# Convolution LayerNorm and swish moved ahead of the output projection, the conv half first, and the first convolution tile as VectorE multiply-adds, in a two-layer hybrid diffusion backbone

## The chip, the cores and the metric

The kernel runs on one core of one Trainium2 chip. The metric is the device time of one execution in microseconds (us); lower is better. Of the kernel before, three runs gave a median of 1693.96 us (1691.78 to 1694.18), and one more execution was profiled.

## The reference

Two layers, each with an attention group and a convolution group side by side, then one output projection and a feed-forward part (SwiGLU). There are 512 latent tokens and 256 context tokens; the second layer updates the latent tokens alone. Cut to what matters here:

```python
h = modulate(rmsnorm(x, g_mix[l]), sh1, sc1)
q, k, v, u = split_in(h @ w_in[l])                    # 512 | 128 | 128 | 1024 columns
q, k = rope_2d(q, ...), rope_2d(k, ...)
a_out = latent_attention(q, k, v, k_c, v_c, sink[l])  # 8 heads, 2 KV heads, window of 128
cv_out = conv_module(u, w_dw[l], b_dw[l], ln_g[l], ln_b[l])
x = x + gt1 * (concat([rmsnorm(a_out, g_a), rmsnorm(cv_out, g_c)]) @ w_o)
h2 = modulate(rmsnorm(x, g_ffn[l]), sh2, sc2)
x = x + gt2 * swiglu(h2, w_gate_up[l], w_down[l])

def conv_module(u, w_dw, b_dw, ln_g, ln_b):           # 512 channels, 31 taps per channel
    z = u[..., :512] * sigmoid(u[..., 512:])
    z = depthwise_conv(z, w_dw) + b_dw
    return silu(layernorm(z, ln_g, ln_b))
```

## The kernel before, in words

Features lie on the 128 partitions and tokens along the free dimension, so a width of 1024 is 8 tiles and the convolution group is 4 tiles (CT). A tile is 768 columns wide in layer 0 (latent and context) and 512 in layer 1. Every float32 product is made of three fp32r matmuls: high weights by high activations, high by low, low by high. ScalarE makes the high part of the weights (`split_high`, L643) and VectorE the low part (`split_low`, L902), both in two buffers; the next block of TensorE needs both. SyncE's queue brings the weights, 512 KB a block.

The order is written out by hand for each engine. Per layer, TensorE (L395) runs these phases:
- **u** (8 blocks), the convolution group's input. VectorE's `u_pair` (L1101) makes the gated z. GpSimd's `shift_z` (L1291) issues 16 DMAs for each tile that lay out shifted copies of z. `conv_tile` (L461) then does the depthwise convolution of a tile as matmuls over those copies. `CONV_AFTER` (L329) puts the four tiles behind u blocks 5, 6 and 7 and qkv block 0. ScalarE copies the sums out with the bias (`conv_copy`, L694).
- **qkv** (6 blocks): keys, four tiles of queries, values. For each, VectorE scales, splits weights and turns (`rope`, L1056), ScalarE copies the high part of the queries (L787, L788), and VectorE subtracts the low part (L1129, L1131).
- **attention** (L518, L700, L996): 48 units (a head by a block of 128 queries) in layer 0 and 32 in layer 1. TensorE computes scores, turns the probabilities and multiplies by the values, ScalarE does the exponential and the copy of the turned probabilities, and VectorE the row maximum and the division.
- **oa** (`out_phase`, L503): 8 tiles of the output projection over the attention half, 4 k-tiles each. The statistics of the convolution's LayerNorm and of both group norms are issued between its tiles (STAT_AFTER, L331). The sums over features are VectorE's (`add_square`, L908), the sums over partitions and the broadcasts are TensorE's (`stat_tokens`, L415, `stat_broadcast`, L423), the root is ScalarE's (L664), the reciprocals on a diagonal are VectorE's (`diagonal`, L922).
- **ob**: the 8 tiles over the convolution half. For oa as for ob, VectorE scales each product by the gate and the group's inverse root (`gate_out`, L985) and GpSimd adds it to x (L1331).
- **gu0, dn0, gu1, dn1, gu2, dn2**: the feed-forward part. The first gu0 block starts on the tiles of x as they become ready and carries the statistics of the norm before it (n2).

`Chain.link` (L119) makes an engine wait for its own last instruction before the next one, which is how dependent VectorE instructions are ordered.

## Time and profile before

| | us |
|---|---|
| median of 3 runs | 1693.96 (1691.78 to 1694.18) |
| profiled execution | 1693.07, of which the traced span is 1691.3 |
| TensorE matmul busy | 1594.6 |
| VectorE, ScalarE, GpSimd busy | 797.1, 571.7, 129.9 |

The mean granted TensorE clock is 0.977 of full speed. In the trace, layer 0 runs u from 52 to about 170 us, qkv to 231, attention to 325.6, oa and ob to 436.9, the feed-forward part to 1031. Layer 1 follows: u to 1099, qkv to 1148, attention to 1224.7, oa and ob to 1300.5, the feed-forward part to the end. PE is the matmul, PEld the weight load, DVE VectorE, ACT ScalarE, POOL GpSimd. In the clock column 1.00 is 2.4 GHz and 0.50 is 1.2 GHz.

### The profile page before, as it was taken

The numbers are of one execution on the slowest core, as the hardware profiler recorded it, in microseconds if no ns is written. First come the engines' busy times: TensorE is split into PE (matmuls) and PEld (weight loads), VectorE is DVE, ScalarE is ACT, GpSimd is POOL, SyncE is SP. The second block draws the span as 40 slices with busy tenths as digits, with TensorE's granted clock in tenths as the row PEclk, the third lists the DMA queues.
The fourth block names the chain that finished last, engine by engine and source line by source line (L and its number), as shares of the span: only waits on it lengthen the run. The fifth ranks groups of instructions, "written<-read, shape, count | busy, mean of one in ns | idle before, by whom it ended". The sixth has DMA issues, their size and how long they took to land.

```text
span 1691.3 us, 25398 instructions
## 1 busy us (share of the span) xinstructions
PE 1594.6 (94%) x9996; PEld 1288.5 (76%) x9996; DVE 797.1 (47%) x1468; ACT 571.7 (34%) x890; POOL 129.9 (8%) x182
## 2 busy tenths in 40 slices
PE   4899989888999999999999999997988999999997
PEld 1666665576788878888788878685566998998995
DVE  1521578786534323343233455267786443443445
ACT  2411257743343211222112233126754541222222
POOL 0133000033100000000000002410032000000000
PEclk9999999998899999999999999998999999999998
DMA  7574420011122432223421354520012323233322
GB/s 317 201 216 128 162 100 2 1 38 38 51 62 62 137 137 100 62 62 134 140 96 63 102 173 150 139 77 29 1 38 63 100 87 99 88 97 90 91 83 87
DMA packets 41180, 165.02 MB, mean 98 GB/s; under 512 B 6160, under 2 KB 6544, under 8 KB 34960
## 3 DMA queue, kind: packets, MB, share of 16 engines
q1 hardware_dynamic: 35856, 148.69, 26.6%
q0 software_dynamic: 5248, 15.27, 3.3%
q8 instruction: 53, 0.87, 0.2%
q14 instruction: 23, 0.19, 0.0%
HBM read 150.77 MB, written 2.10 MB: 90 GB/s over the span
## 4 chain that ended last, share of the span: by engine, by line
PE 82%; DVE 5%; issue 5%; ACT 3%; POOL 3%; DMA 1%; SPq 1%; DVEq 0%; ACTq 0%; POOLq 0%
PE banks L446 66%; PE banks L474 4%; PE banks L546 3%; PE banks L558 2%; PE banks L571 2%; POOL x L1331 2%; PE banks L404 2%; DMA x<-in_xT 1%; DVE ssum L913 1%; PE banks L420 1%; PE banks L433 1%; ACT w_high L650 1%; DVE w_low L906 1%; ACT prob L712 0%; POOL z_shifted L1305 0%
## 5 line engine op out<-in xcount | busy, mean ns | idle before, releaser
L446 PE MATMUL banks<-h_high,w_high 128*128 128x258 f32 (+2 forms) x2048 | 499.9, 323 | 29.4 <-DVE h_low L935 17.6
L446 PE MATMUL banks<-h_low,w_high 128*128 128x258 f32 (+2 forms) x2048 | 491.2, 319 | 0.0
L446 PE MATMUL banks<-h_high,w_low 128*128 128x258 f32 (+2 forms) x2048 | 490.5, 318 | 0.0
L650 ACT ACTIVATE w_high<-raw 128x1024 fp32r<-128x1024 f32 (+1 forms) x178 | 185.1, 1040 | 668.3 <-PE banks L446 660.1
L446 PEld LDWEIGHTS banks<-h_high,w_high 128*128 128x128 f32 x2048 | 323.0, 192 | 79.6 <-issue 41.9
L446 PEld LDWEIGHTS banks<-h_low,w_high 128*128 128x128 f32 x2048 | 322.8, 191 | 28.1 <-issue 0.7
L446 PEld LDWEIGHTS banks<-h_high,w_low 128*128 128x128 f32 x2048 | 322.0, 191 | 27.6
L906 DVE TENSOR_TENSOR w_low<-raw,w_high 128x1024 fp32r<-128x1024 f32 (+1 forms) x178 | 218.2, 1226 | 247.0 <-ACT w_high L650 243.0
L949 DVE COPY shift_product<-banks 128x2 f32<-128x2 f32 x116 | 18.5, 159 | 431.7 <-PE banks L446 407.3
L446 PE MATMUL banks<-ff_high,w_high 128*128 128x512 f32 (+1 forms) x528 | 162.5, 362 | 0.5 <-DVE ff_low L1235 0.5
L446 PE MATMUL banks<-ff_low,w_high 128*128 128x512 f32 (+1 forms) x528 | 160.4, 358 | 0.0
L446 PE MATMUL banks<-ff_high,w_low 128*128 128x512 f32 (+1 forms) x528 | 160.3, 358 | 0.0
L446 PEld LDWEIGHTS banks<-ff_high,w_high 128*128 128x128 f32 x528 | 86.9, 188 | 33.4 <-issue 17.6
L446 PEld LDWEIGHTS banks<-ff_high,w_low 128*128 128x128 f32 x528 | 87.1, 188 | 16.0
L446 PEld LDWEIGHTS banks<-ff_low,w_high 128*128 128x128 f32 x528 | 87.1, 188 | 15.9
L950 DVE TENSOR_TENSOR tmp<-banks,inv_root 128x768 f32<-128x768 f32 (+1 forms) x116 | 95.1, 820 | 0.1
L1331 POOL TENSOR_TENSOR x<-x,tmp 128x768 f32<-128x768 f32 (+1 forms) x32 | 61.2, 1923 | 401.9 <-DVE tmp L992 401.9
L546 PE MATMUL banks<-k_stacked,q_stacked 128*128 128x384 f32 (+2 forms) x224 | 61.9, 383 | 11.9 <-DVE tmp L950 5.7
L1305 POOL DMA_DIRECT2D z_shifted<-z_padded x128 | 62.8, 499 | 130.4 <-issue 54.4
L474 PE MATMUL banks<-z_shifted,w_conv 128*32 128x512 f32 (+1 forms) x768 | 70.4, 521 | 0.8 <-DMA w_conv<-in_w_conv 0.8
L1005 DVE TENSOR_REDUCE row_max<-banks 128x1 f32<-128x512 f32 (+2 forms) x80 | 55.3, 691 | 29.2 <-PE banks L546 28.7
L858 ACT ACTIVATE ff_high<-tmp 128x768 f32 (+3 forms) x44 | 32.5, 740 | 97.9 <-DVE tmp L1231 97.9
(129 smaller groups left out, 1234.5 us busy)
## 6 DMA issues: line engine op xcount, KB each, us to landing
raw<-in_w_gu SPq DMA_DIRECT2D x88, 512.0 KB, 3.6
ada_raw<-in_w_ada SPq DMA_DIRECT2D x21, 1024.0 KB, 5.2
raw<-in_w_dn SPq DMA_DIRECT2D x32, 512.0 KB, 3.6
raw<-in_w_mix SPq DMA_DIRECT2D x28, 512.0 KB, 5.8
ada_in_ff<-in_w_ada SPq DMA_DIRECT2D x12, 1024.0 KB, 5.0
raw<-in_w_out SPq DMA_DIRECT2D x16, 512.0 KB, 3.6
ada_first<-in_w_ada SPq DMA_DIRECT2D x7, 1024.0 KB, 12.9
z_shifted<-z_padded POOLq DMA_DIRECT2D x64, 101.4 KB, 2.7
```

The costliest lines, as they stand in the source:

```text
L404: last = mm(bank[32 * q:32 * q + 32, ADA, :], cond[:, k, :], tile[:, 512 * q:512 * q + 512], start=(k == 0), stop=(k == DT - 1), tile_posi ...
L446: last = mm(bank[:, 2 * slot + bk, 0:b - a], weights[w][:, k0_w + k, :], rhs[:, k0_rhs + k, a:b], start=(k == 0 and n == 0), stop=(k == kt ...
L474: last = mm(bank[QC * q:QC * q + QC, BC + bk, 0:b - a], wD[:, j, g, QC * q:QC * q + QC], zr[j][:, q, SH * g + a:SH * g + b], start=(g == 0 ...
L546: last = mm(wide[:, at:at + w], lhs, rhs, start=in_bank[m] not in in_bank[:m], stop=in_bank[m] not in in_bank[m + 1:], skip_group_check=True)
L558: last = nc.tensor.transpose(wide[:, 512 * PTB + P * m:512 * PTB + P * m + P], probs[u % 4][:, P * m:P * m + P], ident[:])
L571: last = mm(bank[HD * odd:HD * odd + HD, BC + n % 2, 0:2 * P], V[:, keys[m], HD * g:HD * g + HD], PT[:, n % 2, m, 2 * odd:2 * odd + 2, :]. ...
L650: f(wH[j][:, 0:k, :], raw[j][:, 0:k, :], ACT.Copy).then_inc(w_high, 1)
L906: tt(wL[j][:, 0:k, :], raw[j][:, 0:k, :], f32(wH[j][:, 0:k, :]), ALU.subtract).then_inc(w_low, 1)
L950: tt(like(tmp[slot]), src, like(rs), ALU.mult).then_inc(slot_free[slot], 1)
L1005: nc.vector.reduce_max(mx[:, c:c + 1], score_place(u, qs[q][2]), AX.X).then_inc(row_ok, 1)
L1305: pool.dma_start(zr[k % 2][QC * c:QC * c + QC, q, 0:w], z[QC * q:QC * q + QC, k, c:c + w])\
L1331: nc.gpsimd.tensor_tensor(x[:, t, 0:w], x[:, t, 0:w], tmp[t % 2][:, 0:w], ALU.add).then_inc(x_added, 1)
```

## The change

Tile 0 of the convolution leaves TensorE and GpSimd's queue: VectorE does it as 31 dependent multiply-adds for each token stream between the weight splits of u pairs 1 to 3. LayerNorm's mean, centring and variance move from oa into qkv, with the feature sums on GpSimd. Scaling, swish, squares and the high/low split of the convolution half move into attention: scaling by the inverse root and the sum of squares are GpSimd's, swish, squares and high parts ScalarE's (`conv_norm`, called once per unit), low parts VectorE's. The output projection begins with ob, whose operands are then there, and the attention half's norm is made between ob's tiles. oa's operands are normalised beforehand, so VectorE updates x itself, straight from the product, and GpSimd adds nothing in oa. Five new tiles are laid over storage that is free by then. The diff, cut to its core:

```diff
-PHASES = [("u", 4, 8), ("qkv", 3, 8), ("oa", 2, 8), ("ob", 2, 8)]
+PHASES = [("u", 4, 8), ("qkv", 3, 8), ("ob", 2, 8), ("oa", 2, 8)]
...
-        CONV_AFTER = {("u", 5): 0, ("u", 6): 1, ("u", 7): 2, ("qkv", 0): 3}
+        CONV_AFTER = {("u", 6): 1, ("u", 7): 2, ("qkv", 0): 3}
...
             def out_phase(layer, name, blocks):
+                high, low = (conv_high, conv_low) if name == "ob" else (attn_high, attn_low)
...
+                    if name == "ob" and t == 0:
+                        pe.wait_ge(conv_lo, CT * (layer + 1))
+                    tile_product(j, 4 * m, m, CT, high, low, 0, tok_cols(blocks == TB, False),
+                                 (h_ok, h_index[layer, "an"]) if name == "oa" and t == 0 else None)
+                    if name == "ob" and t == 0:
+                        stat_broadcast((layer, "cn"), blocks)
+                    if name == "ob" and t == 2:
+                        stat_tokens((layer, "an"), blocks)
+                    if name == "ob" and t == 4:
+                        stat_broadcast((layer, "an"), blocks)
...
                 for n in range(1, 4):
                     scores(n)
+                stat_broadcast((layer, "var"), blocks)
...
+                        if 2 * i + j == 1:
+                            stat_broadcast((layer, "mean"), blocks)
+                        if 2 * i + j == 4:
+                            stat_tokens((layer, "var"), blocks)
...
-                attention(layer)
-                out_phase(layer, "oa", 0, blocks)
-                out_phase(layer, "ob", 1, blocks)
+                attention(layer, blocks)
+                stat_tokens((layer, "cn"), blocks)
+                out_phase(layer, "ob", blocks)
+                out_phase(layer, "oa", blocks)
...
@@ ScalarE, called after unit n of attention @@
+            def conv_norm(layer, n, width):
+                if n == 0:
+                    act.wait_ge(slot_free[1], USES[layer, "ob"])
+                    copy_root((layer, "var"), width)
+                elif n == 7:
+                    for k in range(CT):
+                        act.wait_ge(ln_y, CT * layer + k + 1)
+                        f(cv[:, k, 0:width], z[:, k, 0:width], ACT.Silu, bias=col("ln_b", k, layer),
+                          scale=col("ln_g", k, layer)).then_inc(ln_s, 1)
+                elif n in (8, 9, 10, 11):
+                    k = n - 8
+                    act.wait_ge(ln_s, CT * layer + k + 1)
+                    square("cn", layer, k, cv[:, k, 0:width])
+                elif n in (12, 13, 14, 15):
+                    k = n - 12
+                    f(conv_high[:, k, 0:width], cv[:, k, 0:width], ACT.Copy, scale=col("g_conv", k, layer)).then_inc(conv_hi, 1)
...
@@ ScalarE, in qkv @@
+                        if t == 2:
+                            for k in range(CT):
+                                act.wait_ge(ln_d, CT * layer + k + 1)
+                                square("var", layer, k, z[:, k, 0:width])
+                        if t == 4:
+                            root((layer, "var"), blocks)
...
@@ ScalarE, oa @@
+                for t in range(DT):
+                    if t % 2:
+                        split_high(layer, "oa", t // 4, t // 2 % 2)
+                    act.wait_ge(slot_free[t % 2], USES[layer, "oa"] + t // 2 + 1)
+                    if t == 1:
+                        shift_high(layer, 3)
+                    high(t, x[:, t, :], gains(layer, 1, context, t))
+                    square("oa", layer, t, x[:, t, 0:width])
...
@@ VectorE, in attention @@
+                    if n in (16, 17, 18, 19):
+                        k = n - 16
+                        dve.wait_ge(conv_hi, CT * layer + k + 1)
+                        stt(out=conv_low[:, k, 0:width], in0=cv[:, k, 0:width], scalar=col("g_conv", k, layer),
+                            in1=f32(conv_high[:, k, 0:width]), op0=ALU.mult, op1=ALU.subtract).then_inc(conv_lo, 1)
...
@@ VectorE, u @@
+                def taps(first, last):
+                    for j in range(first, last):
+                        for a, b, v in streams(context):
+                            at = (CC if v else 0) + j
+                            zt, acc = z[:, 0, at:at + b - a], cv[:, 0, a:b]
+                            if j == 0:
+                                made = ts(acc, zt, col("w_dw", j, layer), col("b_dw", 0, layer), ALU.mult, ALU.add)
+                            else:
+                                made = stt(out=acc, in0=zt, scalar=col("w_dw", j, layer), in1=acc, op0=ALU.mult, op1=ALU.add)
+                        if j == TAPS - 1:
+                            made.then_inc(conv0_ok, 1)
+                        else:
+                            chain.link(made)
...
                     split_low(layer, "u", i, 0)
+                    if i:
+                        taps(10 * i - 10, 10 * i - 5)
...
                     u_pair(i)
+                    if i:
+                        taps(10 * i - 5, 10 * i + (i == 3))
...
@@ VectorE, qkv, behind t == 1 @@
+                            dve.wait_ge(bc_ok, stat_index[layer, "mean"] + 1)
+                            for k in range(CT):
+                                for a, b, _v in streams(context):
+                                    last = stt(out=z[:, k, a:b], in0=wide[:, 512 * BC + a:512 * BC + b], scalar=-1.0 / CW,
+                                               in1=cv[:, k, a:b], op0=ALU.mult, op1=ALU.add)
+                                last.then_inc(ln_d, 1)
+                        if t == 4:
+                            diagonal((layer, "var"), blocks)
...
@@ VectorE, in ob @@
+                    if t == 2:
+                        diagonal((layer, "an"), blocks)
+                    if t == 4:
+                        dve.wait_ge(bc_ok, stat_index[layer, "an"] + 1)
+                        for k in range(CT):
+                            stt(out=aT[:, k, 0:width], in0=aT[:, k, 0:width], scalar=col("g_attn", k, layer),
+                                in1=wide[:, 512 * BC:512 * BC + width], op0=ALU.mult, op1=ALU.mult).then_inc(an_ok, 1)
+                    if t == 6:
+                        for k in range(CT):
+                            dve.wait_ge(high_ok, h_index[layer, "an"] + k + 1)
+                            tt(attn_low[:, k, 0:width], aT[:, k, 0:width], f32(attn_high[:, k, 0:width]),
+                               ALU.subtract).then_inc(h_ok, 1)
@@ VectorE, oa @@
+                for t in range(DT):
+                    dve.wait_ge(gemm, 2 * USES[layer, "oa"] + t + 1)
+                    dve.wait_ge(x_added, DT * layer + t + 1)
+                    update(layer, t % 2, USES[layer, "oa"] + t // 2, 2, t, context)
...
@@ GpSimd @@
+                for k in (1, 2):
                     load_conv(layer, k)
+                for k in (1, 2, 3):
+                    shift_z(layer, k)
+                    if k == 3:
+                        load_conv(layer, k)
...
+                pool.wait_ge(bc_ok, stat_index[layer, "mean"] + 1)
+                sum_squares("var")
+                pool.wait_ge(rs_ok, rs_index[layer, "var"] + 1)
                 for k in range(CT):
+                    nc.gpsimd.tensor_tensor(z[:, k, 0:w], z[:, k, 0:w], rs[:, 0:w], ALU.mult).then_inc(ln_y, 1)
+                pool.wait_ge(tok_mm, root_index[layer, "var"] + 1)
+                sum_squares("cn")
```

Before `sum_squares("var")`, GpSimd also adds the four convolution tiles for the mean. `sum_squares` adds the first two squares in one instruction, then the third and the fourth.

## Rows read from the trace of the kernel before

**Rows 1.** The page's busy times by engine

```profile
PE 1594.6 (94%) x9996; PEld 1288.5 (76%) x9996; DVE 797.1 (47%) x1468; ACT 571.7 (34%) x890; POOL 129.9 (8%) x182
```

**Rows 2.** Busy time by stretch: length, PE, PEld, DVE, ACT, POOL, clock, DMA

```profile
325.60:437.00 111.40, 93.06 (x461) 76.90 (x461) 83.02 (x127) 49.20 (x72) 35.87 (x16) 0.89 0.12 35
1225.00:1300.50 75.50, 61.32 (x248) 45.73 (x248) 57.73 (x88) 37.84 (x58) 25.34 (x16) 0.91 0.16 50
235.00:325.00 90.00, 84.32 (x518) 52.22 (x517) 69.35 (x256) 68.46 (x194) 0.00 (x0) 0.96 0.02 7
1154.00:1224.00 70.00, 66.41 (x422) 42.64 (x420) 51.34 (x168) 52.49 (x131) 0.00 (x0) 0.94 0.03 9
```

**Rows 3.** Chain of waits around both output projections (start, length, what)

```profile
325.12 0.43 DVE attn_out L1035
...
436.85 4.22 PE banks L446 x12
...
1300.55 3.12 PE banks L446 x24
```

**Rows 4.** Chain inside layer 0's attention, 262 to 280 us, by line

```profile
by line: PE banks L571 36.0%; PE banks L558 30.7%; PE banks L546 25.7%; issue 3.2%; ACT prob L712 3.1%; ACT esink L714 1.1%; ACT probT L724 0.2%; ACTq L723 0.1%
```

**Rows 5.** Chain in the u phases: convolution tile, then block, layers 0 and 1

```profile
111.94 10.33 PE banks L474 x121
...
1066.25 7.01 PE banks L474 x64
1073.26 5.92 PE banks L446 x48
```

**Rows 6.** VectorE in time order, qkv of layer 1

```profile
1130.20 1.22 DVE L906 TENSOR_TENSOR w_low<-raw,w_high 128x1024 fp32r<-128x1024 f32 x1
...
1132.87 0.74 DVE L1072 SCALAR_TENSOR_TENSOR tmp<-tmp,shift_product,cosT 128x512 f32<-128x512 f32 x1
1133.64 0.69 DVE L1074 TENSOR_TENSOR tmp<-tmp,sq 128x512 f32<-128x512 f32 x1
```

**Rows 7.** VectorE in time order: GpSimd adds beside the first two

```profile
343.39 2.03 DVE L906 TENSOR_TENSOR w_low<-raw,w_high 128x1024 fp32r<-128x1024 f32 x1
345.35 3.80 DVE L1175 SCALAR_TENSOR_TENSOR z_padded<-banks,conv 128x512 f32<-128x512 f32 x8
```

**Rows 8.** ScalarE in time order: table load and exponential, two squares, a swish

```profile
238.23 1.28 ACT L712 ACT_TABLE_LOAD   x1
239.53 0.69 ACT L712 ACTIVATE prob<-banks,neg_max 128x512 f32<-128x512 f32 x1
...
329.64 1.56 ACT L662 ACTIVATE sq<-attn_out 128x768 f32<-128x768 f32 x2
...
370.68 0.94 ACT L823 ACTIVATE conv<-z_padded,par 128x768 f32<-128x768 f32 x1
```

**Rows 9.** ScalarE's idle time in one attention unit, in brackets

```profile
264.98 0.70 ACT L724 ACTIVATE probT<-banks 128x640 f32<-128x640 f32 x1 [0.42 <-PE banks L558]
```

**Rows 10.** PE alone in stretches of 2 us: length, busy, clock, DMA

```profile
383.00:385.00 2.00, 0.00 (x0) 0.93 0.00 0
385.00:387.00 2.00, 1.16 (x3) 0.50 0.00 0
...
445.00:447.00 2.00, 2.00 (x8) 0.50 0.00 0
```

**Rows 11.** PE: a 36-matmul tile of 512 and 256 columns; k-steps of 512

```profile
974.26 6.54 PE banks L446 x36
...
L446 PE MATMUL banks<-ff_high,w_high x64: 393/395/398, 1392.2 to 1436.3; 128*128 128x512 f32 x64
```

**Rows 12.** PE in time order: statistics between tiles, layer 0

```profile
334.96 1.50 PE L420 MATMUL banks<-mean_col,ssum 128*128 128x1 f32 x12
...
338.57 1.12 PE L433 MATMUL banks<-diagonals,ones 128*128 128x512 f32 x2
```

**Rows 13.** GpSimd in time order: an add in layer 0

```profile
409.46 2.50 POOL L1331 TENSOR_TENSOR x<-x,tmp 128x768 f32<-128x768 f32 x1 [4.97 <-DVE tmp L992]
```

233 lines of the change are left out of this document (101 added, 132 removed).

## The prediction

> **What bounds the kernel now.** I read the page first: matmuls fill 94% of the span [rows 1], so a microsecond counts only where TensorE (PE) is paced or left waiting. The view by stretches comes next. The two output projections are long for what they hold: 111.4 us in layer 0 with 93.1 busy at a clock of 0.89, and 75.5 us in layer 1 with 61.3 busy at 0.91 [rows 2]. The chain of waits gives their ends: attention's last copy starts at 325.12, gu0's first matmul at 436.85, and in layer 1 at 1300.55 [rows 3]. In between the chain runs through VectorE, ScalarE and GpSimd. The attentions (90 and 70 us) are the opposite: all three engines are busy together, DVE 77%, ACT 76%, PE 94% [rows 2], and the chain inside is almost all PE (L571, L558, L546) [rows 4]. So PE paces attention, but ScalarE has only 0.42 us idle in a unit of about 1.9 us [rows 9]. In u, PE works without a gap; a convolution tile is a plain link of the chain [rows 5].
>
> **u: convolution tile 0 leaves PE.** It took 10.33 us in layer 0 and 7.01 in layer 1 [rows 5]. In exchange VectorE gets 31 dependent multiply-adds per stream. A dependent 512-column step costs 0.77 us (1132.87 to 1133.64) [rows 6]; a pair of 512 and 256 columns costs 0.95 (3.80 for eight pieces [rows 7]), with the dependent wait 1.05 to 1.15. Five taps are 5.6 us in layer 0 and 3.9 in layer 1. Beside them a block needs about 2.3 to 2.5 us (product, 1.22 for the split [rows 6]) and every second one 0.8 to 1.2 more for z. That is 8.1 and 9.3 us against PE's 9.6 a block with its adaLN matmuls in layer 0, and 6.2 and 7.0 against 5.92 [rows 5] in layer 1. There VectorE falls behind by 1.3 us a pair, 2.6 in all until tile 1's matmuls give it 7 us; the double-buffered weights allow about 5.9 - 2.2 = 3.7. So the taps cost nothing, and if that cover is gone the next block waits for its low weights. The last six taps run beside tile 2's matmuls. GpSimd's queue drops 16 DMA issues and a weight load, but tile 3's stay where they were, so its wait stays too. **Gain: 10.3 and 7.0.**
>
> **qkv.** VectorE gets the centring, 3.80 us in layer 0 [rows 7] and about 2.7 in layer 1, and the diagonal, 1.4 and 1.1. ScalarE gets four squares between the query copies and the next weight split. A square is 0.8 us at 768 columns (1.56 for two) [rows 8], and the third waits for GpSimd's add of the first two, 2.50 [rows 13]; with the split behind them VectorE waits 3.3 us for its high weights, 2.5 in layer 1. GpSimd's adds stretch VectorE: the same split took 2.03 us beside one and 1.22 alone [rows 6, 7]; I add 1.5 and 1. In layer 0 VectorE idles some 2.8 us over these blocks, which pays part of it back. Together 3.8 + 3.3 + 1.4 + 1.5 - 2.8 = 7.2, and 2.7 + 2.5 + 1.1 + 1 = 7.3 in layer 1, which has no idle time. PE's mean broadcast and variance tokens go beside this. **Cost: 7 and 7.5**; bounds 4 and 5 (all in idle time) to 11 and 10 (with stretched rope steps).
>
> The trace agrees here with the Trainium skill (GPSIMD Engine Reference, Key points): GpSimd shares its SBUF interfaces with VectorE instructions that have two SBUF inputs.
>
> **Attention.** Each addition is weighed against ScalarE's 0.42 us.
> - The variance broadcast stands in PE's own order, where the clock is at 1.2 GHz: 2 us in layer 0, 1.1 in layer 1. The inverse root's copy adds 0.3.
> - Unit 7 gets a burst: a table load for swish (1.28), four swishes at 0.94, less 0.09 overlap each, and a load back for the exponential (1.28) [rows 8]: 6.0 us, in layer 1 four of 0.65 and so 5.1. PE can go on for one unit, about 1 us. That leaves 5.0 and 4.1.
> - After such a gap PE comes back at 1.2 GHz: idle at 383, clock 0.50 from 385 on [rows 10]. I take 2.5 us for each.
> - Units 8 to 11 get a square each (0.75 against 0.42, and one wait for GpSimd): 1.6 and 0.2. Units 12 to 15 get a high part each: 2.0 and 1.2. Units 16 to 19 get a low part on VectorE: 2.2 and 0.8.
>
> Sum: 2 + 0.3 + 5.0 + 2.5 + 1.6 + 2.0 + 2.2 = 15.6, and 1.1 + 0.3 + 4.1 + 2.5 + 0.2 + 1.2 + 0.8 = 10.2. **Cost: 15.5 and 10.** Lower bounds 8 and 6 (the burst alone, clock kept), upper 28 and 20 (nothing absorbed, the low clock lasting as long as at 445, ten microseconds after the gap there [rows 10]). I take the values near the low end because PE stands in the chain there with ScalarE idle in each unit [rows 4, 9].
>
> The row of the load before the exponential ends at 239.51 and the exponential starts at 239.53 [rows 8], so a switch costs its 1.28 us here. The Trainium skill (ScalarE: Activation LUTs, What ACT_TABLE_LOAD costs) puts a switch at 2.66 us with a drain; by it the four switches would cost 5.5 us more, and the row shows no such gap, so I give it no weight.
>
> **The output projection, layer 0.** PE goes on without a gap: both operands of ob are there. A tile is 24 matmuls of 512 or 256 columns; 36 take 6.54 us at full clock [rows 11], so 4.36, and 16 tiles take 69.8. Two token sums at 1.4 (1.50 less overlap) and two broadcasts at 1.2 [rows 12] make 5.2. The first root and diagonal end about 4.7 us after attention, before tile 0 does (5.8). VectorE needs some 22 us in the 39 of ob, and about 3.9 a tile in oa against 4.36 (update 1.1, half a split 0.6, square sum 1.0, low part 1.2); GpSimd 2.5 [rows 13] of 4.36. I allow 3 us for handovers: 78.0 instead of 111.3 (325.56 to 436.85 [rows 3]). **Gain 33.3.** Then gu0: its first block ran at 0.50 up to 447 [rows 10], after PE had idled. Now its first six k-steps are ready when oa ends. **Gain 4.5**; bounds 0 to 5.
>
> **Layer 1.** 64 k-steps of three matmuls take 44.1 us, 0.70 each [rows 11]; a tile is 2.80 and 16 are 44.8. Statistics 3.4, allowance 3: 51.2 instead of 75.9. **Gain 24.7.** Per oa tile VectorE has 2.8 of work against 2.80, so this is tight. If every handover of oa's came late by half a microsecond a tile, it would be 4 us a layer; bounds of the two gains together are 45 and 62.
>
> **Sum.** -10.3 - 7.0 + 7 + 7.5 + 15.5 + 10 - 33.3 - 4.5 - 24.7 = -39.8. The profiled execution took 1693.07 us (span 1691.3), 0.9 under the median, so 1653.3 for it and 1654 beside the median.
>
> **The rivals.**
> - *Attention pays the upper bound.* Work put into a stage where three engines are three quarters full is not absorbed, the queue order makes each extra ScalarE instruction a PE gap, and the clock falls more than once. For it: 0.42 us of slack [rows 9]; against: the added work, some 13 us, is under ScalarE's 21 us idle in 90 [rows 2]. Attention then costs 28 and 20, 22.5 more: 1677.
> - *oa turns into a VectorE-bound phase.* The chain from update over high part, low part and square sum is paced by the slower engine, and PE idles and drops its clock as it does at 385 [rows 10]. For it: 2.8 against 2.80 in layer 1; against: GpSimd's add has left that chain. Half the projection gain is lost, 29 us: 1683.
> - *The taps do not fit (the slower side).* If a dependent tap with two SBUF inputs costs what a split costs beside GpSimd, 1.65 times its row [rows 6, 7], it is 1.85 in layer 0 and 1.3 in layer 1. Blocks then take 11.8 and 13.0 against 9.6, and 8.8 and 9.6 against 5.92: over three pairs some 17 and 20 us. With that lateness qkv starts late on VectorE, where layer 1 has no idle time, another 6: 1697. It decides for slower from about 1.8 and 1.3 us a tap. Against: GpSimd only issues DMAs there, and the rope rows show 0.77.
> - *Attention absorbs the small pieces.* Only the broadcast and the burst remain: 12 us less, 1642.
> - *The change doesn't do what it says:* only if the projection keeps waiting for something late, such as the low part of the convolution half; those are made 28 units before the end in layer 0, so I give this 1 in 100.
>
> **How the numbers follow.** Forecast 0.63, own range 1641 to 1668 (terms at moderate distance in their bounds), attention dear 0.17, oa bound 0.09, absorbed 0.04, taps 0.06, no effect 0.01. The likeliest is 1654. The range 1636 to 1682 takes in the upper attention case and half of the oa case, with just under 2 in 10 outside. About 0.2% (3.4 us) is what a measurement of this kernel can tell from no change: faster 0.89, same 0.04, slower 0.07.
>
> **What would show it.** In the changed profile, PE in u goes from block to block with two convolution tiles fewer over the layers and no wait for w_low; taps take 0.77 us in layer 1. The chain in qkv runs through VectorE with a wait for w_high behind the third block. In attention one PE gap of 5 us stands at unit 7, with clock 0.50 behind it, and the stage takes about 105 and 80 us. From attention's last matmul to gu0's first it is 78 and 51 us at clock 1.00. It is wrong if attention grows by over 20 us a layer, if PE waits for DVE h_low or the slot in oa on each tile, or if u shrinks by less than 8 and 5 us.

## The result and the profile after

The changed kernel takes **1656.3 us** (median of four runs, 1651.8 to 1658.4) against 1694.0 before: a ratio of 0.9777, with a 95% interval of 0.9755 to 0.9799. The forecast was 1654 with a range of 1636 to 1682. The profiled execution has a span of 1656.1 us and a mean granted clock of 0.981 (before 0.977). Run again beside the last experiments, the same kernel gave 0.9767 (0.9747 to 0.9787).

The page's busy line and the chain by engine, of the kernel after, beside [rows 1]:

```profile
PE 1570.3 (95%) x9804; PEld 1278.1 (77%) x9804; DVE 837.1 (51%) x1527; ACT 570.1 (34%) x882; POOL 126.3 (8%) x162
...
PE 84%; DVE 7%; ACT 4%; issue 2%; DMA 2%; SPq 1%; POOL 0%; DVEq 0%; ACTq 0%; POOLq 0%
```

PE lost 24 us of busy time in all: two convolution tiles, and low-clock time and statistics in the output projections, less what low clock and statistics added in qkv and the attentions. VectorE took on 40 us. To see where the 35.2 us of span went I cut both traces at the same instructions: the first matmul of convolution tile 3, the first score matmul, the end of the last values matmul, the end of the n2 broadcast inside gu0, and, where layer 1 begins, the first token sum of its first norm.

| stage | before | after | difference | forecast |
|---|---|---|---|---|
| up to tile 3, layer 0 (u) | 172.0 | 162.7 | -9.3 | -10.3 |
| qkv, layer 0 | 62.6 | 68.9 | +6.3 | +7 |
| attention, layer 0 | 90.5 | 109.3 | +18.8 | +15.5 |
| output projection and start of gu0, layer 0 | 126.0 | 85.6 | -40.4 | -37.8 |
| rest of the feed-forward part, layer 0 | 581.9 | 582.8 | +0.9 | 0 |
| u, layer 1 | 75.6 | 70.8 | -4.8 | -7.0 |
| qkv, layer 1 | 44.9 | 52.9 | +8.0 | +7.5 |
| attention, layer 1 | 70.7 | 80.5 | +9.8 | +10 |
| output projection and start of gu0, layer 1 | 83.4 | 58.2 | -25.2 | -24.7 |
| rest, layer 1 | 383.7 | 384.2 | +0.5 | 0 |

The view by stretches (length, PE, PEld, DVE, ACT, POOL busy, clock, DMA), cut as in the table. The projections before, which [rows 2] show up to gu0 alone:

```profile
325.10:451.10 126.00, 107.15 (x507) 88.57 (x508) 88.89 (x142) 50.88 (x75) 35.87 (x16) 0.85 0.11 34
...
1224.20:1307.60 83.40, 68.37 (x302) 52.30 (x303) 61.95 (x98) 38.87 (x59) 25.34 (x16) 0.92 0.17 51
```

and all four stages after:

```profile
231.60:340.90 109.30, 93.02 (x525) 56.15 (x523) 78.05 (x260) 82.55 (x210) 13.32 (x8) 0.91 0.02 5
340.90:426.50 85.60, 85.50 (x487) 73.66 (x488) 61.20 (x102) 31.50 (x47) 19.19 (x8) 1.00 0.16 50
1133.00:1213.50 80.50, 71.15 (x424) 44.84 (x424) 57.50 (x172) 64.54 (x148) 9.38 (x8) 0.92 0.03 8
1213.50:1271.70 58.20, 58.17 (x291) 47.76 (x290) 47.02 (x72) 24.03 (x38) 11.63 (x8) 1.00 0.24 73
```

The projections are now solid: 85.50 us busy of 85.60 and 58.17 of 58.20, at clock 1.00. Before, PE idled 19 and 15 us in them, and the busy time itself was longer at clocks of 0.85 and 0.92. What went away there stands in the view of waits before, PE, 325 to 451 us (in total, times, longest):

```profile
PE banks L446 <- DVE h_low L935: 9.4, 4, 3.2
PE banks L433 <- DVE diagonals L928: 3.9, 2, 2.0
PE banks L446 <- DVE tmp L992: 3.0, 3, 2.2
```

After, the same view of the same stage has one wait alone, the 0.5 us with which attention ends. The attentions pay. Cut in the same way, layer 0's had 84.79 us of PE time in 90.50 before: now it has 8.2 us more of it (lower clock, an added broadcast) and 10.6 us more idle time.

The chain of waits of the kernel after (start, length, what):

```profile
122.49 10.32 PE banks L494 x124
...
202.44 1.59 ACT sq L696 x2
...
204.19 1.89 POOL ssum L1390
...
206.91 0.83 ACT sq L696
207.74 0.96 ACT w_high L684
...
208.72 1.24 DVE w_low L949
```

In u it still goes from PE block to PE block. In qkv it runs as forecast: two squares, GpSimd's add of them, the other squares, the high weights, the low weights. At the end of qkv PE waits 5.1 us for ScalarE's copy of the adaLN row (L722), against 1.9 before (L688), since all of ScalarE's and VectorE's queue has moved later.

### The profile page after: what moved, and what is told of

It is laid out like the page before. It is cut to its first block, busy times and chain, and to the rows that moved or that the text cites. A ratio compares the mean times of both kernels' runs of the same rounds, so it can differ in the third digit from the quotient of the medians.

```text
span 1656.1 us, 25043 instructions
## 1 busy us (share of the span) xinstructions
PE 1570.3 (95%) x9804; PEld 1278.1 (77%) x9804; DVE 837.1 (51%) x1527; ACT 570.1 (34%) x882; POOL 126.3 (8%) x162
## 4 chain that ended last, share of the span: by engine, by line
PE 84%; DVE 7%; ACT 4%; issue 2%; DMA 2%; SPq 1%; POOL 0%; DVEq 0%; ACTq 0%; POOLq 0%
PE banks L465 71%; PE banks L494 3%; PE banks L572 2%; PE banks L584 2%; PE banks L599 2%; PE banks L412 2%; DMA x<-in_xT 1%; PE banks L452 1%; PE banks L435 1%; DVE w_low L949 1%; ACT prob L765 1%; DVE ssum L956 1%; DMA raw<-in_w_mix 0%; ACT w_high L684 0%; DVE row_max L1048 0%
## 5 line engine op out<-in xcount | busy, mean ns | idle before, releaser
L465 PE MATMUL banks<-h_high,w_high 128*128 128x512 f32 (+1 forms) x1856 | 433.3, 315 | 5.0 <-DVE h_low L978 3.5
L465 PE MATMUL banks<-h_high,w_low 128*128 128x512 f32 (+1 forms) x1856 | 428.8, 313 | 0.0
L465 PE MATMUL banks<-h_low,w_high 128*128 128x512 f32 (+1 forms) x1856 | 428.6, 312 | 0.0
L465 PEld LDWEIGHTS banks<-h_high,w_high 128*128 128x128 f32 x1856 | 289.0, 190 | 40.1 <-issue 18.8
L465 PEld LDWEIGHTS banks<-h_low,w_high 128*128 128x128 f32 x1856 | 288.4, 190 | 21.6
L465 PEld LDWEIGHTS banks<-h_high,w_low 128*128 128x128 f32 x1856 | 287.3, 190 | 21.6
L1024 DVE SCALAR_TENSOR_TENSOR x<-banks,mod,x 128x512 f32 (+1 forms) x96 | 60.3, 656 | 11.1 <-PE banks L465 11.0
L1287 DVE TENSOR_TENSOR ff_low<-tmp,ff_high 128x768 f32 (+3 forms) x44 | 36.3, 826 | 43.7 <-ACT ff_high L901 43.7
L777 ACT ACTIVATE probT<-banks 128x512 f32<-128x512 f32 (+2 forms) x80 | 48.0, 600 | 29.2 <-PE banks L584 28.7
```

The lines of the kernel that those rows point to most:

```text
L465: last = mm(bank[:, 2 * slot + bk, 0:b - a], weights[w][:, k0_w + k, :], rhs[:, k0_rhs + k, a:b], start=(k == 0 and n == 0), stop=(k == kt ...
L777: f(PT[:, group % 2, 0:w, i % 2 * 2 + i // 2, :], wide[:, 512 * PTB:512 * PTB + P * w].rearrange("p (k q) -> p k q", k=w), ACT.Copy).then_ ...
L1024: last = stt(out=xt, in0=bank[:, 2 * slot + (a >= N), 0:b - a], scalar=mod[:, layer, bass.ds(t + gate * DT, 1), v], in1=xt, op0=ALU.mult, ...
L1287: tt(aL[:, i, 0:width], tmp[1][:, 0:width], f32(aH[:, i, 0:width]), ALU.subtract).then_inc(ff_low, 1)
```

## Experiments

All ratios are to the kernel before, measured beside it on the same chip; stage lengths are cut as above.

| run | u, qkv, attention, projection (layer 0) | the same, layer 1 | median us | ratio (95%) |
|---|---|---|---|---|
| before | 172.0, 62.6, 90.5, 126.0 | 75.6, 44.9, 70.7, 83.4 | 1693.96 | 1 |
| changed | 162.7, 68.9, 109.3, 85.6 | 70.8, 52.9, 80.5, 58.2 | 1656.3 | 0.9777 (0.9755 to 0.9799) |
| e1_tile0_on_pe | 171.9, 68.8, 108.7, 85.6 | 78.8, 52.3, 80.3, 58.2 | 1674.66 | 0.9892 (0.9875 to 0.9908) |
| e7_gpsimd_adds | 161.4, 68.8, 108.7, 97.2 | 69.3, 52.9, 80.5, 67.4 | 1675.31 | 0.9888 (0.9867 to 0.9909) |
| e8_more_taps | 162.3, 68.8, 106.7, 85.6 | 70.5, 52.3, 82.7, 58.2 | 1656.95 | 0.9783 (0.9759 to 0.9807) |
| e5_squares_later | 162.2, 66.7, 107.3, 85.6 | 67.6, 52.8, 79.8, 58.2 | 1653.43 | 0.9769 (0.9751 to 0.9788) |
| e2_scale_on_dve | 162.3, 68.7, 104.9, 85.6 | 70.8, 52.9, 79.9, 58.2 | 1649.57 | 0.9741 (0.9725 to 0.9758) |
| e3_no_swish_table | 162.1, 68.7, 103.4, 85.6 | 67.7, 52.9, 75.7, 58.2 | 1645.04 | 0.9708 (0.9688 to 0.9728) |
| e4_pe_busy | 161.0, 68.8, 106.6, 87.1 | 70.8, 52.9, 79.3, 58.2 | 1655.38 | 0.9770 (0.9749 to 0.9790) |
| e6_spread | 160.9, 68.9, 105.5, 85.6 | 67.6, 52.9, 79.3, 58.2 | 1651.48 | 0.9750 (0.9725 to 0.9774) |
| changed, again | 162.0, 69.3, 108.4, 85.6 | 67.6, 52.9, 81.6, 58.2 | 1655.98 | 0.9767 (0.9747 to 0.9787) |
| e9_three_together | 162.3, 66.8, 102.1, 85.6 | 67.6, 52.6, 78.6, 58.2 | 1643.28 | 0.9691 (0.9672 to 0.9711) |
| e10_tanh | 162.7, 66.9, 96.6, 86.6 | 67.5, 52.8, 71.9, 58.2 | 1626.99 | 0.9597 (0.9574 to 0.9619) |

The changed kernel's attention differs by up to 1.1 us between its profiles (109.3, 108.4 and 80.5, 81.6), and parts of it by more. Attention's code is the same in the changed kernel, e1, e3, e4, e6, e7 and e8 up to ScalarE's copy of the turned probabilities of unit 7 (it starts at 261.12 in the first profile of the changed kernel). From the first score matmul to that copy, layer 0 took 29.6 us in that profile and 29.3 in e1, but 27.2 to 27.5 in the six other profiles: the clock was at 1.2 GHz for 6.8 us there in the first two, for 3.4 us or not at all in the others. So some 2 us of every difference from 109.3 come by chance. Layer 1 took 24.0 to 25.8 us up to that copy. Behind it, the profiles with the changed kernel's attention (changed twice, e1, e5, e7, e8) took 79.3 to 81.2 us in layer 0 and 55.6 to 56.8 in layer 1; the edits below that act only behind unit 7 are weighed against these. Layer 1's u varies too (67.6, 69.3 or 70.8 us with the same code), told of at the end.

### The convolution tile back on TensorE

```diff
-        CONV_AFTER = {("u", 6): 1, ("u", 7): 2, ("qkv", 0): 3}
+        CONV_AFTER = {("u", 5): 0, ("u", 6): 1, ("u", 7): 2, ("qkv", 0): 3}
...
-                    if i:
-                        taps(10 * i - 10, 10 * i - 5)
...
-                    if i:
-                        taps(10 * i - 5, 10 * i + (i == 3))
```

> The changed kernel with one part undone: convolution tile 0 is matmuls on TensorE again, behind u block 5, with its 16 shift DMAs and weight load on GpSimd's queue; VectorE makes no taps. Theory (the taps are covered): u grows by one tile in each layer, 10.3 and 7.0 us, and nothing else moves: 1656 + 17 = 1673. Rival (the taps cost VectorE time that PE waits for): u gives less back, the whole grows by under 12 us, 1668 or less. Rival 2: tile 0 had slack of its own in layer 1, since u there only shrank by 4.8 us with the change, part of it a low clock at its start: then layer 1 grows by under 5 us.

u grew by 9.2 and 8.0 us (in layer 1 both profiles have the low clock at the start, so the second rival is out) and nothing else moved by more than 0.6; the whole is 1674.66 against 1656.3. So tile 0's move is worth what its matmuls took, 17 us over the layers, and the 31 taps that replace them cost nothing that shows.

### Fifteen more taps

```diff
                             chain.link(made)
+                            if j % 2:
+                                for a, b, v in streams(context):
+                                    at = (CC if v else 0) + j
+                                    dummy = stt(out=scratch[:, a:b], in0=z[:, 0, at:at + b - a], scalar=col("w_dw", j, layer),
+                                                in1=cv[:, 0, a:b], op0=ALU.mult, op1=ALU.add)
+                                chain.link(dummy)
```

> The changed kernel with 15 extra dependent multiply-adds among the 31 taps, each for both streams into a scratch tile whose result is not used: VectorE's work in u is half as large again, 2.2 us more per block in layer 0 and 1.6 in layer 1. Theory (the cover is what PE's block leaves: 9.6 us in layer 0, 5.92 in layer 1 with 3.7 us of double buffering): layer 0 loses about 3 us a pair less what the buffers allow, some 4; layer 1 lags 4.5 us a pair and loses 6 to 8: 1667. Rival (the taps have far more room than counted): under 2 us. Rival 2 (they were at the limit already): over 16 us.

The dummy results are thrown away. In layer 0 u did not grow (162.3 against 162.7). In layer 1 it took 70.5 us at clock 1.00 where the changed kernel takes 67.6 at that clock: 2.9 us more for 11.7 us of VectorE work (15 times 0.78). The whole, 1656.95, cannot be told from the changed kernel, where I had expected 1667. The view of waits, PE, layer 1's u of this run, and below it the real taps in the time order of VectorE of the changed kernel:

```profile
PE banks L494 <- DMA w_conv<-in_w_conv: 1.3, 1, 1.3
PE banks L465 <- DVE w_low L949: 1.2, 1, 1.2
```

```profile
1037.51 3.90 DVE L1161 SCALAR_TENSOR_TENSOR conv<-z_padded,par,conv 128x512 f32<-128x512 f32 x5
```

A tap takes 0.78 us, as forecast from the rope rows (0.77). My reckoning that the buffers give 3.7 us of room was too tight: half as many taps again add nothing in layer 0 and about 3 us in layer 1, of which 1.2 are the wait for the low weights and 1.3 one for the weights of convolution tile 3, which the changed kernel's second profile does not have.

### The additions of the second projection back on GpSimd

```diff
-                    dve.wait_ge(x_added, DT * layer + t + 1)
-                    update(layer, t % 2, USES[layer, "oa"] + t // 2, 2, t, context)
+                    dve.wait_ge(x_added, 2 * DT * layer + DT + t - 1)
+                    for a, b, v in streams(context):
+                        last = ts(tmp[t % 2][:, a:b], bank[:, 2 * (t % 2) + (a >= N), 0:b - a],
+                                  mod[:, layer, 2 * DT + t, v:v + 1], None, ALU.mult)
+                    last.then_inc(slot_free[t % 2], 1)
...
-                for t in range(DT):
-                    pool.wait_ge(slot_free[t % 2], USES[layer, "ob"] + t // 2 + 1)
+                for name, t in [(name, t) for name in ("ob", "oa") for t in range(DT)]:
+                    pool.wait_ge(slot_free[t % 2], USES[layer, name] + t // 2 + 1)
```

> The changed kernel with one part of the projection undone: in oa VectorE only scales the product by the gate into tmp and GpSimd adds it to x, as before, instead of VectorE updating x itself. Theory (the chain gate, GpSimd, ScalarE and the stretch of VectorE beside GpSimd were what made the projection long): per tile VectorE's 3.9 us become 4.8 to 5 against PE's 4.36 in layer 0 and 2.8 become 3.7 against 2.80 in layer 1, and the tail before gu0 grows by GpSimd's 2.5 and 1.7 us: 6 to 9 us in each layer, 1668 to 1674. Rival (the gain came from ob's operands being ready and from the norms' chain being out of the way; GpSimd's add is hidden): only the tail, 2 to 4 us in all, 1659.

The projections grew by 11.6 and 9.2 us, more than the 6 to 9 expected: 29% of the gain in layer 0 and 37% in layer 1 hang on this one part of the change. The other parts (ob's operands ready at its start, the norms' chain out of the way) no run undid; for them the views of waits before and after stand alone. The views of time order (VectorE) and of waits (PE) of this run:

```profile
388.76 2.01 DVE L949 TENSOR_TENSOR w_low<-raw,w_high 128x1024 fp32r<-128x1024 f32 x1 [1.00 <-ACT w_high L684]
...
394.32 2.73 DVE L978 SCALAR_TENSOR_TENSOR h_low<-x,gain,h_high 128x512 fp32r<-128x512 f32 x2
```

```profile
PE banks L435 <- DVE row_max L963: 4.8, 1, 4.8
PE banks L465 <- DVE tmp L1256: 2.4, 2, 1.7
```

and the same two VectorE rows in the changed kernel:

```profile
389.66 1.23 DVE L949 TENSOR_TENSOR w_low<-raw,w_high 128x1024 fp32r<-128x1024 f32 x1
...
394.74 1.14 DVE L978 SCALAR_TENSOR_TENSOR h_low<-x,gain,h_high 128x512 fp32r<-128x512 f32 x2
```

VectorE instructions with two SBUF inputs are stretched beside GpSimd's additions, from 1.23 to 2.01 and from 1.14 to 2.73 us. In the chain of 378 to 420 us the additions are 40.7%; 54.7% are time for which the view names no cause. At the stretch's end the statistics of n2 come late: PE waits 4.8 us for them, and the clock falls to 1.2 GHz at 424.

### The four squares of qkv a step later

```diff
+                        if t == 3:
+                            for k in range(CT):
+                                act.wait_ge(ln_d, CT * layer + k + 1)
+                                square("var", layer, k, z[:, k, 0:width])
...
-                        if t == 2:
-                            for k in range(CT):
-                                act.wait_ge(ln_d, CT * layer + k + 1)
-                                square("var", layer, k, z[:, k, 0:width])
```

> The changed kernel, but ScalarE's four squares for the variance come behind the weight split of the fourth qkv block instead of ahead of it. Theory (in qkv VectorE waits for the high weights that stand behind the squares in ScalarE's queue): the wait of 3 us in each layer goes and the squares fall into ScalarE's idle time while VectorE turns the queries; qkv shrinks by 3 us in layer 0 and 2.5 in layer 1: 1651. Rival (what then comes last is the sum for the variance: PE waits longer for GpSimd's sum before block 5): no gain, 1656.

qkv fell by 2.2 us in layer 0 and by 0.1 in layer 1; in the whole the run cannot be told from the changed kernel. The wait for the high weights is gone in layer 0, but GpSimd's add now stands beside a rope step. VectorE of this run:

```profile
209.42 2.23 DVE L1122 TENSOR_TENSOR tmp<-tmp,diagonals 128x512 f32<-128x512 f32 x1
```

The same addition takes 0.69 us alone [rows 6], so 1.5 us of the gain went to contention. In layer 1 the rival came true. The view of waits, PE, qkv of layer 1 of this run:

```profile
PE banks L435 <- POOL sum_mark L1398: 6.9, 1, 6.9
```

The same wait is 5.5 us in the changed kernel, beside a chain that runs over VectorE; here the chain itself goes from the squares through GpSimd's sum to PE, so the later squares only made that sum later.

### LayerNorm's scaling on VectorE instead of GpSimd

```diff
-                pool.wait_ge(rs_ok, rs_index[layer, "var"] + 1)
-                for k in range(CT):
-                    nc.gpsimd.tensor_tensor(z[:, k, 0:w], z[:, k, 0:w], rs[:, 0:w], ALU.mult).then_inc(ln_y, 1)
...
+                    if n in (-1, 0, 1, 2):
+                        k = n + 1
+                        if k == 0:
+                            dve.wait_ge(bc_ok, stat_index[layer, "var"] + 1)
+                        tt(z[:, k, 0:width], z[:, k, 0:width], wide[:, 512 * BC:512 * BC + width], ALU.mult).then_inc(ln_y, 1)
```

> The changed kernel, but the scaling of z by LayerNorm's inverse root is VectorE's, one tile after each of units -1 to 2, straight from the broadcast in PSUM, instead of GpSimd's four multiplies and ScalarE's copy of the root. In the changed kernel's profile VectorE's one-column add (psums) lasts 1.8 us instead of 0.15 beside these multiplies. Theory (GpSimd holds the interface that VectorE needs, and that stalls attention): the long adds vanish, VectorE pays 4 x 0.95 us and 4 x 0.7 us, partly in its own idle time, PE's gaps around units 1 to 4 and the low clock after them go; attention shrinks by 4 to 8 us in layer 0 and 2 to 4 in layer 1: 1645 to 1650. Rival (the stretch is in VectorE's idle time anyway): no change within 2 us, 1656. Rival 2 (VectorE is the fuller engine): 2 to 4 us slower, 1659.

Attention fell by 4.4 us in layer 0 and by 0.6 in layer 1, though VectorE does more. Not all of it is the edit's: up to unit 7's copy layer 0 took 25.0 us, 2.2 to 2.5 less than the six profiles without the long fall of the clock, and behind it 79.9, inside the 79.3 to 81.2 above; in layer 1 nothing clear is left. That is under the 4 to 8 and 2 to 4 us of the theory, and the interval of the whole overlaps the changed kernel's. What the edit removes stands in the time order of the changed kernel, GpSimd's row first and then VectorE's:

```profile
244.88 7.59 POOL L1404 TENSOR_TENSOR z_padded<-z_padded,inv_root 128x768 f32<-128x768 f32 x4 [32.90 <-ACT inv_root L705]
```

```profile
244.75 0.15 DVE L1061 TENSOR_TENSOR psums<-psums,esink 128x1 f32<-128x1 f32 x1
...
246.90 1.80 DVE L1061 TENSOR_TENSOR psums<-psums,esink 128x1 f32<-128x1 f32 x1
```

An addition of one column per partition takes 0.15 us, and 1.8 us beside GpSimd's multiplies (a second one, at 250.71, took 1.78), close to the 1.9 us of one of them (7.59 for four). PE waits 2.1 us for VectorE at 250.84. In the run with the multiplies on VectorE:

```profile
241.39 0.95 DVE L1095 TENSOR_TENSOR z_padded<-z_padded,banks 128x768 f32<-128x768 f32 x1 [0.60 <-PE banks L454]
242.26 0.15 DVE L1058 TENSOR_TENSOR psums<-psums,esink 128x1 f32<-128x1 f32 x1
```

They cost 0.95 us each there, the small addition is back at 0.15, and the mean clock of the stretch's first 31 us is 0.89 instead of 0.77 (0.84 in the changed kernel's second profile, so a part of this is the chance named above).

### The burst: without its tables, with PE kept busy, and the rest spread out

Three runs on what unit 7's burst costs. The first leaves swish out (a plain copy with scale and bias), so that neither table load is needed:

```diff
-                        f(cv[:, k, 0:width], z[:, k, 0:width], ACT.Silu, bias=col("ln_b", k, layer),
+                        f(cv[:, k, 0:width], z[:, k, 0:width], ACT.Identity, bias=col("ln_b", k, layer),
```

> The changed kernel without swish: ScalarE's four instructions of unit 7 apply the identity with the same scale and bias (left out: the swish of the convolution half), so that no table is loaded ahead of them and none behind. Theory (the burst's price is its length, with 1.28 us a load as in the rows, and the low clock that follows the gap): 2.6 us less in each layer by length; if the gap left over (2.4 us) still lets the clock fall, 5 us in all, 1651; if the clock now stays, 4 to 5 us a layer, 1647. Rival (the loads fall into ScalarE's idle time): under 2 us in all.

Attention fell by 5.9 and 4.8 us, but a part of this stands ahead of unit 7, where the edit can do nothing yet. Behind unit 7's copy it took 76.0 and 51.6 us: 3.3 to 5.2 and 4.0 to 5.3 less than the profiles with the same attention, against 2.57 for the two loads themselves. So some 1 to 3 us a layer go with them beyond their length; the low clock behind the burst lasts 3.4 us in layer 0 instead of 6.8 to 10.2, and does not come in layer 1. The burst in ScalarE's time order, in the changed kernel:

```profile
261.12 0.70 ACT L777 ACTIVATE probT<-banks 128x640 f32<-128x640 f32 x1 [0.49 <-PE banks L584]
...
262.81 1.28 ACT L743 ACT_TABLE_LOAD   x1
264.10 3.79 ACT L743 ACTIVATE conv<-z_padded,par 128x768 f32<-128x768 f32 x4
...
268.50 1.28 ACT L765 ACT_TABLE_LOAD   x1
269.79 0.79 ACT L765 ACTIVATE act_out<-banks,neg_max 128x640 f32<-128x640 f32 x1
```

The load ends at 269.78 and the exponential starts at 269.79: as in [rows 8], no drain beyond the load's own time shows.

The second run fills PE's gap with matmuls whose result nobody reads:

```diff
+                    if n == 9:
+                        pe.wait_ge(a_ok, group_index[layer, 0] + 1)
+                        for _ in range(18 if layer == 0 else 14):
+                            mm(bank[:, BC, 0:N], Q2[:, 0, 0:P], K2[:, 0, 0, 0:N], start=True, stop=True)
```

> The changed kernel with 18 (layer 0) and 14 (layer 1) extra matmuls of 512 columns into a free bank ahead of unit 9's turn, where PE waits for the burst; their results are not used. Theory (after the gap PE comes back at 1.2 GHz and that costs 2 to 2.5 us a layer beyond the gap): granted clock 1.00 behind the burst and 4 to 5 us less in all, 1652. Rival (in these microseconds ScalarE sets the pace, not PE's clock): the clock stays and the time does not change, 1656.

PE in stretches of 2 us (length, busy, clock), in the changed kernel:

```profile
252.00:254.00 2.00, 1.33 (x8) 0.59 0.04 8
...
266.00:268.00 2.00, 0.00 (x0) 1.00 0.00 0
268.00:270.00 2.00, 0.74 (x5) 0.85 0.00 0
270.00:272.00 2.00, 1.09 (x3) 0.50 0.00 0
```

and in this run:

```profile
266.00:268.00 2.00, 1.49 (x10) 1.00 0.00 0
...
270.00:272.00 2.00, 1.95 (x14) 1.00 0.00 0
```

The clock stays at 2.4 GHz through the burst. Attention is 2.7 and 1.2 us shorter than in the changed kernel's first profile, but in layer 0 2.3 of that stand ahead of unit 7's copy; behind it the run took 79.3 us, as long as the fastest profiles without the extra matmuls, and 54.4 in layer 1, 1.2 less than they. The projection of layer 0 loses 1.5, and the whole cannot be told from the changed kernel: the rival holds. After the burst PE waits 1.1 us for ScalarE's copy at 273.62, a wait that the changed kernel does not have: a PE at full clock mostly waits for ScalarE sooner.

The third takes the squares and the high and low parts two units apart instead of one:

```diff
-                elif n in (8, 9, 10, 11):
-                    k = n - 8
+                elif n in (8, 10, 12, 14):
+                    k = (n - 8) // 2
...
-                elif n in (12, 13, 14, 15):
-                    k = n - 12
+                elif n in (16, 18, 20, 22):
+                    k = (n - 16) // 2
...
-                    if n in (16, 17, 18, 19):
-                        k = n - 16
+                    if n in (21, 23, 25, 27):
+                        k = (n - 21) // 2
```

> The changed kernel, but squares come after units 8, 10, 12, 14, high parts after 16, 18, 20, 22, low parts after 21, 23, 25, 27: one piece every second unit instead of every unit. Theory (each piece costs what it exceeds the idle time of a unit, 0.42 us for ScalarE): spread out, two units' idle time covers one piece, and most of the 5.8 us (layer 0) and 2.2 us (layer 1) that I put on them goes: 1650. Rival (each piece stops PE for what it lasts beyond one slack, whatever its distance to the next): no change, 1656.

Attention fell by 3.8 and 1.2 us, of which 2.3 and 0.9 stand ahead of unit 7's copy and are not the edit's. Behind it the run took 78.3 and 55.4 us, 1.0 to 3.0 and 0.2 to 1.5 less than the profiles with the same attention; the whole cannot be told from the changed kernel. The sign is that of the theory, that the same instructions cost less when each has a free unit behind it, but its size is not shown, and it is well under the 5.8 us put on the pieces in layer 0.

### Together, and swish from the exponential's table

The ninth run has the edits of e2, e5 and e6 in one kernel. The tenth adds to it a swish without a table of its own: with w half the scaled and shifted value, swish is w (1 + tanh w). VectorE makes w and the product, ScalarE the tanh, one tile every second unit:

```diff
-                if n == 7:
-                    for k in range(CT):
-                        act.wait_ge(ln_y, CT * layer + k + 1)
-                        f(cv[:, k, 0:width], z[:, k, 0:width], ACT.Silu, bias=col("ln_b", k, layer),
-                          scale=col("ln_g", k, layer)).then_inc(ln_s, 1)
...
+                if n in (5, 7, 9, 11):
+                    k = (n - 5) // 2
+                    act.wait_ge(w_ok, CT * layer + k + 1)
+                    f(cv[:, k, 0:width], z[:, k, 0:width], ACT.Tanh).then_inc(t_ok, 1)
...
+                    if n in (3, 5, 7, 9):
+                        k = (n - 3) // 2
+                        dve.wait_ge(ln_y, CT * layer + k + 1)
+                        ts(z[:, k, 0:width], z[:, k, 0:width], halved[:, layer, k:k + 1], halved[:, layer, CT + k:CT + k + 1],
+                           ALU.mult, ALU.add).then_inc(w_ok, 1)
+                    if n in (7, 9, 11, 13):
+                        k = (n - 7) // 2
+                        dve.wait_ge(t_ok, CT * layer + k + 1)
+                        stt(out=cv[:, k, 0:width], in0=cv[:, k, 0:width], scalar=1.0, in1=z[:, k, 0:width],
+                            op0=ALU.add, op1=ALU.mult).then_inc(ln_s, 1)
```

> The changed kernel with three edits that each gained alone: z scaled by VectorE, the variance's squares behind the fourth weight split, and one piece every second unit. By stages the three took 4.4, 2.2 and 3.8 us off layer 0 and 0.6, 0.1 and 1.2 off layer 1. Theory (they act in different places: units 1 to 4, qkv, units 8 to 19): they add up, some 12 us, 1644. Rival (attention is then paced by one full engine, so that the second saving finds no gap left): as good as the best alone, 1650.

> The previous kernel, with swish made without a table switch: half the argument w on VectorE, tanh(w) on ScalarE, one tile after units 5, 7, 9 and 11, and w (1 + tanh w) on VectorE, so that no burst is left in unit 7. Leaving the switches out alone took 5.9 us off attention in layer 0 and 4.8 in layer 1. Theory (tanh is taken from the table that the exponential has loaded, and single pieces are covered by idle time): the gap and the low clock behind it go, four more VectorE pieces of about 0.95 and 0.5 us per layer cost 2 to 3 us a layer: 5 to 8 us less than the previous kernel, 1637. Rival 1 (tanh needs a table of its own): eight more loads a layer, 15 us or more slower. Rival 2 (VectorE becomes the bound of attention, with 5.8 us more in layer 0): no gain.

> The changed kernel once more, on the chip of the two kernels before, so that they can be compared in the same call: 1656 by its first runs, a ratio of 0.978 to the kernel before; layer 1's first block with its clock at 1.00 or at 0.50, 3.2 us apart, by chance from run to run.

Three together: 0.9691, clear of the changed kernel's 0.9767 beside it. The sum of 12 us came true in the whole (12.7), though 2 us of the 4.4 and of the 3.8 were the same chance: against the changed kernel's second profile, qkv fell by 2.5 and 0.3 us and the attentions by 6.3 and 3.0. With tanh: **0.9597 (0.9574 to 0.9619), 1626.99 us**, the fastest version; it beats the changed kernel by 29 us and the kernel before by 69 (1695.77 beside it). Its attentions take 96.6 and 71.9 us, 5.5 and 6.7 less than in the ninth run, all but 0.2 of it behind unit 7's copy. ScalarE there, then the stretch of layer 0's attention:

```profile
251.94 0.83 ACT L742 ACTIVATE conv<-z_padded 128x768 f32<-128x768 f32 x1
252.68 0.69 ACT L775 ACTIVATE probT<-banks 128x640 f32<-128x640 f32 x1
253.26 0.79 ACT L763 ACTIVATE prob<-banks,neg_max 128x640 f32<-128x640 f32 x1
```

```profile
224.00:320.00 96.00, 84.35 (x510) 51.77 (x509) 84.41 (x270) 76.91 (x201) 5.65 (x4) 0.96 0.02 6
```

Tanh and exponential follow each other with no load between, and the clock is back at 0.96, the value of [rows 2]. The Trainium skill (ScalarE: Activation LUTs, Table sets: the hidden batching unit) says that exp and then tanh need one load; the trace agrees, with one load a layer at the exponential's line instead of two there and one at swish's. Not explained: this run's feed-forward stages were 3.0 and 1.5 us shorter than the ninth's, though their code is the same; so 4.5 of the 16.3 us between the two are not shown to be tanh's.

## Why the prediction was right, and where its steps were not

**The output projection** was right in mechanism and in sum (-40.4 and -25.2 for -37.8 and -24.7), but two errors in it cancel. I took 436.85 for gu0's first matmul, and the stage times ahead of the prediction end the projection there too. In the time order of PE before:

```profile
429.47 0.59 PE L446 MATMUL banks<-h_high,w_high 128*128 128x512 f32 x2 [0.41 <-DVE tmp L992]
...
436.85 0.80 PE L446 MATMUL banks<-h_high,w_high 128*128 128x512 f32 x1 [2.93 <-DVE h_low L935]
441.09 2.72 PE L420 MATMUL banks<-mean_col,ssum 128*128 128x1 f32 x12
```

and after:

```profile
413.81 0.53 PE L465 MATMUL banks<-h_high,w_high 128*128 128x512 f32 x2
...
420.43 1.50 PE L435 MATMUL banks<-mean_col,ssum 128*128 128x1 f32 x12
```

The sums over tokens stand behind gu0's sixth k-step in both. Before, only two k-steps lie between 436.85 and them: gu0 had begun at 429.47, run four k-steps and waited for the fifth's operand. So I subtracted a time up to the first k-step (78.0) from one up to the fifth (111.3), which overstates the gain by four k-steps, 4.4 us (24 matmuls, by [rows 11]). Against this, the new projection took 72.9 us (340.88 to 413.81), not 78.0: the tiles take 69.8, and my 3 us for handovers and part of the statistics were not needed. Layer 1 has the same slip: gu0 began at 1294.86, not at 1300.55, and the new projection took 48.4 us for my 51.2. That the sums fit so closely is luck. What is left of the gain lies in gu0's start, 21.6 us before (429.47 to 451.04) and 12.7 after, twice the 4.5 I gave it.

**u** was right: -9.3, and -8.0 in layer 1 with the clock alike; the taps cost nothing (e1). The rival in which they do not fit needed 1.65 times the row, 1.3 us a tap in layer 1, and the tap took 0.78 us; with half as many taps again (e8) layer 1 loses 2.9 us, and layer 0 nothing.

**qkv** was right at +6.3 and +8.0 for 7 and 7.5, through the forecast chain. Two things there were not foreseen. PE waits 5.5 us in layer 1 for GpSimd's sum before it can make the variance's token sums; the chain runs over VectorE there, but e5 shows that this sum is next in line. And the root brings a table load of its own into the stage: in the chain at the end of layer 1's qkv it takes 1.28 us (from 1129.23 on), a term that my sum for the diagonal (1.1) left out. The sum's own terms make 7.3 in layer 1, for which I wrote 7.5.

**Attention** was mis-sized by 3.3 us in layer 0 (18.8 for 15.5) and right in layer 1 (9.8 for 10), there in its terms too: 5.7 us more idle time of PE for 6.6, 4.1 more busy time for 3.6. In the other profiles with the same attention (e1, e7, e8, changed again) layer 0's grew by 16.2 to 18.2. PE's waits inside layer 0's attention, by the view of waits (in total, times, longest), after:

```profile
PE banks L584 <- ACT probT L777: 5.8, 6, 4.0
PE banks L572 <- ACT esink L767: 4.5, 5, 2.2
PE banks L584 <- DVE prob L1071: 3.6, 3, 2.1
PE banks L599 <- ACT probT L777: 0.5, 1, 0.5
```

They are 14.4 us against 4.4 before, 10.0 more; the forecast had 11.1 of such terms (5.0 + 0.3 + 1.6 + 2.0 + 2.2). PE's busy time is 8.2 more, where I had 4.5 (2.5 for the clock, 2 for the broadcast). So the term that was too small is "I take 2.5 us for each" low clock: the clock fell twice, at 252 as well as at 269, for 6.8 us each time. The first fall is partly chance: with the same code in attention up to there, it lasted 6.8 us in two of nine profiles, 3.4 us in four and did not come in three (e3, e5, e8), though e3 has the same wait of PE in front of it (2.1 us); in e2, without that wait, it does not come. The long one costs some 2 us. I had put contention with GpSimd into qkv and none into attention, where four of its multiplies hold up VectorE, then PE (3.6 us for DVE prob, 2.8 of them beside the multiplies or just behind; 0.2 before). The rival of the upper bound named the right sign, a clock that falls more than once, at about a quarter of its price in layer 0 (3.3 of 12.5 us) and at none in layer 1.

**oa as a VectorE-bound phase** did not happen: the clock stays 1.00 and PE waits for nothing in layer 0's projection. e7 shows how near it is: with GpSimd's additions back in that chain, 21 of the 66 us are lost.

## What to carry to other kernels

Work moved out of a stage where PE idles can be worth its wait and the low clock behind it even if it goes into a nearly full stage: here the projections gave 65.6 us, and qkv and the attentions, where the work went, took 42.9. Compute it there from the tables that are already loaded (e10), rather than in a burst with loads of its own. One small piece per unit with a free unit between is what the fastest version does, but alone it was not clear of noise (e6). GpSimd's two-input operations are best kept away from stretches in which PE waits for small VectorE steps: there VectorE doing the work itself (0.95 us) was cheaper than GpSimd doing it beside it, by some 2 us in layer 0. When subtracting two stage times, cut both traces at the same instruction; when crediting an edit with a stage's difference, cut the stage where the edit begins to act, and look whether the part ahead of it moved too.

## What the hardware showed that was not expected

- A VectorE addition of a single column (0.15 us) took 1.80 us beside a GpSimd multiply of 768 columns: not a stretch in proportion to its size, but a wait about as long as the GpSimd instruction (1.8 to 2.1 us each). In layer 1, beside multiplies of 512 columns (1.3 to 1.5 us), the same addition took 1.23.
- The start of layer 1 has two courses with the same code, and one between (e7, low for 3.4 us): in the first profile of the changed kernel the clock is low for some 7 us from 1010 on, in the second it stays at 1.00. A stretch of each:

```profile
1010.00:1012.00 2.00, 2.00 (x11) 0.53 0.00 0
```

```profile
1008.00:1012.00 4.00, 3.88 (x31) 1.00 0.00 0
```

It is worth 3.2 us (u of 70.8 and 67.6 us): with the low clock the conv tile's move gives 4.8 us there, without it 8.0, and the forecast's 7.0 lies between. What decides it stays open, as it does for the fall at 252 in layer 0's attention, where the same code had three courses.
- Keeping PE busy through a gap held the clock, and yet was worth nothing measurable in the whole (0.9770 against 0.9777): in these microseconds ScalarE, not PE's clock, set the pace.
